# Two transformer blocks on one core: when the scatter of an expert's output runs among the next experts' matmuls

## The chip, the cores and the metric

The kernel runs on one core of one Trainium2 chip. Its time is that of one execution on the device, in microseconds. Three executions were timed; the trace is of the one that took longest.

## What is computed

Two blocks in a row work on 256 tokens of width 1024, all in float32. The first has two mixers and a mixture of 16 experts, the second attention and two dense feed-forward parts. Only the experts matter here:

```python
for e in range(N_EXPERTS):                  # 16
    a = jax.nn.silu(t @ w_gate[e]) * (t @ w_up[e])
    y = y + combine[:, e:e + 1] * (a @ w_down[e]).astype(f32)
```

`t` is 256 × 1024, `w_gate[e]` and `w_up[e]` are 1024 × 512, `w_down[e]` is 512 × 1024. Each token is routed to 2 of the 16 experts; `combine` is zero for the others.

## The kernel before

**Precision.** A float32 product is made of products of parts. Each weight is split into `w_hi` (rounded, by ScalarE, `split_hi`) and `w_lo` (the rest, by VectorE, `split_lo`); activations are split in the same way.

**Units.** Weights arrive in units of 128 × 2048 values (1 MB) in one order: per expert two for the gate, two for up, and two for down, which stand one expert later. `w_raw` has 6 buffers, `w_hi` and `w_lo` have 3 each (`SPLIT`). So ScalarE can split a unit only when TensorE has used the unit three before it (`unit_used`). TensorE then waits for `lo_ready`.

**Few tokens.** Where every expert has at most 64 tokens the kernel takes the branch `few_experts`, and it does so here. Per expert 64 columns of tokens are gathered, and their high and low parts stand side by side, so that a unit (`unit_few`) is eight matmuls of 128 × 128 by 512: four with `w_hi` (line 1922) and four with `w_lo` (line 1923).

**One pass of the loop on TensorE**, for expert `e`, in order:

1. four units, gate, gate, up, up (called here the first to the fourth unit);
2. the fold of the gate rows (line 1948), which turns them and adds their two parts;
3. the first half of the down product of expert `e-1`, one unit;
4. the fold of the up rows;
5. the transposes that make `pickT` and the weights of `e` (lines 1940 and 1942), and a gather (line 1934) for later experts;
6. the second half of the down product of `e-1`, one unit, which waits until VectorE has read the first half from the same PSUM bank (`y_half_lo`);
7. another gather, and then the scatter of `e-1`.

The scatter (`scatter`, line 1968) multiplies the output rows of an expert, `y_hi` and `y_lo`, by `pickT` and adds them to the tokens' sums in four PSUM banks. It is two halves of four matmuls by 512 columns. Each half waits for `y_half_lo` of its half.

**The other engines.** ScalarE and VectorE have written-out orders of their own, `few_experts` too. On ScalarE, behind the second down unit of `e-1`: `y_hi` of its second half (line 726), the split of the next expert's third unit (line 505), `aT_hi` (line 715), the copy of the gathered rows (line 692). The next pass's first unit waits for that copy (`gath_set`). On VectorE `y_lo` (line 1311) stands between two splits (line 898). `y_hi` and `y_lo` have one buffer for each half: the scatter of `e-1` must be over before the first down unit of `e`, whose end lets ScalarE write them again.

Of the kernel before, what the change touches and what calls it, by code (L numbers as in the profile page):

```python
# [32 lines left out]
N_EXP = GROUPS * PER_GROUP  # L33
# [78 lines left out]
def two_blocks_kernel(nc, a, out):  # L112
# [7 lines left out]
    with ExitStack() as ctx:  # L120
# [76 lines left out]
        def pair_rows(e):  # L197

            buf = h_hi if (e // 2) % 2 == 0 else h_lo
            return buf[:, :, :].rearrange("p k (e m) -> p k e m", e=2)[:, :, e % 2, :]  # L200
# [10 lines left out]
        def u_in(e, j):  # L211
            return U_MOE + j if e == 0 else U_MOE + 4 + STEP * (e - 1) + j
# [1419 lines left out]
        def _(pe):  # L1632
# [284 lines left out]
            def unit_few(u, bank, rows, k0, first, last):  # L1917

                pe.wait_ge(lo_ready, u + 1)
                for k in range(4):  # L1920
                    wc = slice(k * 512, k * 512 + 512)
                    pe.matmul(ps[:, bank, :], rows[:, k0 + k, :], w_hi[:, u % SPLIT, wc], start=first and k == 0, stop=False)  # L1922
                    ins = pe.matmul(ps[:, bank, :], rows[:, k0 + k, :], w_lo[:, u % SPLIT, wc], start=False, stop=last and k == 3)  # L1923
                ins.then_inc(unit_used, 1)

            def gather(n):

                pair = pick[:, :, 2 * (n // 4):2 * (n // 4) + 2, 0:SLOTS]
                for k in range(2):
                    o = ps[:, chunk_bank(n), 256 * k:256 * k + 256].rearrange("p (e l s) -> p l e s", e=2, l=2)  # L1930
                    c = slice((2 * (n % 4) + k) * P, (2 * (n % 4) + k + 1) * P)
                    for part, h2 in enumerate((h2_hi, h2_lo)):
                        for tt in range(TT):
                            ins = pe.matmul(o[:, part], h2[:, tt, c], pair[:, tt], start=(tt == 0), stop=(tt == 1))
                ins.then_inc(gathered, 1)

            def transpose_pick(e):

                for tt in range(TT):
                    pe.transpose(ps[:, B_GATE, tt * P:(tt + 1) * P], pick_f[:, tt, e, :], ident)  # L1940
                for tt in range(TT):
                    ins = pe.matmul(ps[:, B_GATE, S:S + 1], pick_f[:, tt, e, :], comb[:, tt, e:e + 1], start=(tt == 0), stop=(tt == 1))
                ins.then_inc(pick_T, 1)

            def fold_rows(rows, c0):

                for f in range(4):
                    ins = pe.matmul(ps[:, B_T, c0 + SLOTS * f:c0 + SLOTS * (f + 1)], rows[:, f * P:(f + 1) * P], fold, start=True, stop=True)  # L1948
                ins.then_inc(aT_done, 1)

            def down_few(e, half):

                if half:
                    pe.wait_ge(y_half_lo, 2 * e + 1)
                else:
                    pe.wait_ge(aT_lo_r, 2 * (e + 1))
                    if e:
                        pe.wait_ge(y_half_lo, 2 * e)
                unit_few(u_down(e, half), B_Y, aT_hi[:, :, 0:P], 0, True, True)

            def scatter(e, half):

                pe.wait_ge(y_half_lo, 2 * e + (half + 1))
                pe.wait_ge(pickT_set, e + 1)
                for tt in range(TT):
                    o = ps[:, 4 + 2 * half + tt, :]
                    for n, y in enumerate((y_hi, y_lo)):
                        ins = pe.matmul(o, pickT[:, e, tt * P:(tt + 1) * P], y[:, 512 * half:512 * half + 512],  # L1968
                                        start=(e == 0 and n == 0), stop=(e == N_EXP - 1 and n == 1), skip_group_check=True)
                ins.then_inc(y_used, 1)  # L1970

            def few_experts():

                pe.wait_ge(h2_lo_set, 2)
                pe.wait_ge(fold_set, 1)
                pe.wait_ge(pick_ready, 1)
                for n in range(4):
                    gather(n)
                for e in range(N_EXP):
                    rows = pair_rows(e)  # L1980
                    if e == 0:
                        pe.wait_ge(gath_set, 2)
                    else:
                        pe.wait_ge(gath_set, 4 + 2 * min(e, N_EXP - 2))
                        pe.wait_ge(pickT_set, e)
                        pe.wait_ge(slot_w_set, e)
                    unit_few(u_in(e, 0), B_GATE, rows, 0, True, False)
                    if e == 0:
                        pe.wait_ge(gath_set, 4)
                    unit_few(u_in(e, 1), B_GATE, rows, 4, False, True)  # L1990
                    unit_few(u_in(e, 2), B_UP, rows, 0, True, False)
                    unit_few(u_in(e, 3), B_UP, rows, 4, False, True)
                    if e:
                        pe.wait_ge(a_done, e)
                    pe.wait_ge(gate_kept, e + 1)
                    fold_rows(gate_rows, 0)
                    if e:
                        down_few(e - 1, 0)
                    pe.wait_ge(up_kept, e + 1)
                    fold_rows(up_rows, 4 * SLOTS)  # L2000
                    if e == 0:
                        pe.wait_ge(pick_ready, 2)
                    transpose_pick(e)
                    if e < N_EXP - 2:
                        gather(4 + 2 * e)
                    if e:
                        down_few(e - 1, 1)
                    if e < N_EXP - 2:
                        pe.wait_ge(pickT_set, e + 1)
                        pe.wait_ge(slot_w_set, e + 1)  # L2010
                        gather(5 + 2 * e)
                    if e:
                        scatter(e - 1, 0)
                        scatter(e - 1, 1)
                down_few(N_EXP - 1, 0)
                down_few(N_EXP - 1, 1)
                scatter(N_EXP - 1, 0)
                scatter(N_EXP - 1, 1)
# [5 lines left out]
            with pe.If(is_few > 0):  # L2024
                few_experts()
# [326 lines left out]
```

## Time and profile before

| | us |
|---|---|
| three timed runs | 1186.71, 1187.0, 1191.82 |
| their median | 1187.0 |
| the profiled execution, one of the three | 1191.82 |
| its span in the profile | 1189.8 |
| TensorE busy | 1082.2 (91%) |
| VectorE busy | 733.6 (62%) |
| ScalarE busy | 616.8 (52%) |
| mean granted TensorE clock, share of full | 0.945 |

The span is the time from the first to the last instruction that the profiler recorded. Times in the trace count from its start. The stage of the experts lies from about 280 to 604 us. TensorE's busy time counts each matmul from its start to its modelled end, and matmuls overlap: one of 512 columns is shown with 0.39 us, while the next starts 0.23 us after it. So distances from start to start say more than busy time. In the timeline PE is a matmul, PEld the load of its stationary operand, and the bracket gives how long the engine was idle before it and what ended that.

### The profile page before, as it was taken

The numbers are of one execution on the slowest core, as the hardware profiler recorded it, in microseconds if no ns is written. First come the engines' busy times: TensorE is split into PE (matmuls) and PEld (weight loads), VectorE is DVE, ScalarE is ACT, GpSimd is POOL, SyncE is SP. The second block draws the span as 40 slices with busy tenths as digits, with TensorE's granted clock in tenths as the row PEclk, the third lists the DMA queues.
The fourth block names the chain that finished last, engine by engine and source line by source line (L and its number), as shares of the span: only waits on it lengthen the run. The fifth ranks groups of instructions, "written<-read, shape, count | busy, mean of one in ns | idle before, by whom it ended". The sixth has DMA issues, their size and how long they took to land.

```text
span 1189.8 us, 14176 instructions
## 1 busy us (share of the span) xinstructions
PE 1082.2 (91%) x5471; PEld 897.4 (75%) x5471; DVE 733.6 (62%) x821; ACT 616.8 (52%) x721; POOL 56.4 (5%) x47
## 2 busy tenths in 40 slices
PE   5999999887999999999869999987999799999997
PEld 4788888676777777777657888876878677788886
DVE  5434685557678787878764655554556645555654
ACT  5466533345777877777644334333554425344331
POOL 0000561020000000000000000000000000000000
PEclk8999998887999999999889999997998969999999
DMA  7843442343789898989848556552520015555520
GB/s 265 300 142 110 138 142 89 123 149 111 277 319 325 313 336 306 340 306 341 303 152 302 191 181 201 187 177 71 175 73 2 1 36 172 182 178 192 193 72 36
DMA packets 116993, 223.34 MB, mean 188 GB/s; under 512 B 6402, under 2 KB 12681, under 8 KB 116938
## 3 DMA queue, kind: packets, MB, share of 16 engines
q1 hardware_dynamic: 112846, 216.77, 53.0%
q10 hardware_dynamic: 3708, 4.57, 1.1%
q0 software_dynamic: 384, 1.24, 0.3%
q8 instruction: 38, 0.62, 0.2%
q14 instruction: 17, 0.14, 0.0%
HBM read 221.49 MB, written 1.07 MB: 187 GB/s over the span
## 4 chain that ended last, share of the span: by engine, by line
PE 75%; DVE 13%; ACT 7%; issue 3%; ACTq 1%; DMA 0%; DVEq 0%
PE ps L1650 17%; PE ps L1651 16%; PE ps L1652 16%; DVE w_lo L898 7%; PE ps L1922 5%; ACT w_hi L505 4%; PE ps L1923 4%; PE ps L1948 2%; PE ps L2155 2%; PE ps L1968 2%; PE ps L1792 1%; DVE y_lo L1311 1%; ACT y_hi L726 1%; PE ps L2118 1%; DVE h_lo L925 1%
## 5 line engine op out<-in xcount | busy, mean ns | idle before, releaser
L898 DVE TENSOR_TENSOR w_lo<-w_raw,w_hi 128x2048 fp32r<-128x2048 f32 x204 | 465.3, 2290 | 170.6 <-ACT w_hi L505 169.4
L505 ACT ACTIVATE w_hi<-w_raw 128x2048 fp32r<-128x2048 f32 x204 | 388.1, 1913 | 257.1 <-PE ps L1652 208.4
L1650 PE MATMUL ps<-w_hi,h_hi 128*128 128x512 f32 (+1 forms) x704 | 276.0, 392 | 13.4 <-DVE h_lo L925 7.7
L1651 PE MATMUL ps<-w_lo,h_hi 128*128 128x512 f32 (+1 forms) x704 | 271.3, 385 | 0.0
L1652 PE MATMUL ps<-w_hi,h_lo 128*128 128x512 f32 (+1 forms) x704 | 271.2, 385 | 0.0
L1650 PEld LDWEIGHTS ps<-w_hi,h_hi 128*128 128x128 f32 x704 | 135.3, 192 | 41.6 <-DVE h_lo L925 8.6
L1652 PEld LDWEIGHTS ps<-w_hi,h_lo 128*128 128x128 f32 x704 | 134.8, 191 | 26.5
L1651 PEld LDWEIGHTS ps<-w_lo,h_hi 128*128 128x128 f32 x704 | 135.1, 192 | 24.5
L1650 PE MATMUL ps<-w_hi,aT_hi 128*128 128x512 f32 x192 | 77.3, 403 | 7.7 <-DVE aT_lo L1223 6.0
L1651 PE MATMUL ps<-w_lo,aT_hi 128*128 128x512 f32 x192 | 76.7, 400 | 0.0
L1652 PE MATMUL ps<-w_hi,aT_lo 128*128 128x512 f32 x192 | 76.6, 399 | 0.0
L1922 PE MATMUL ps<-w_hi,aT_hi 128*128 128x512 f32 x128 | 54.5, 426 | 9.6 <-DVE y_lo L1311 8.3
L1922 PE MATMUL ps<-w_hi,h_hi 128*128 128x512 f32 x128 | 53.7, 419 | 6.6 <-DVE w_lo L898 5.9
L1922 PE MATMUL ps<-w_hi,h_lo 128*128 128x512 f32 x128 | 51.8, 405 | 5.8 <-DVE w_lo L898 5.8
L1923 PE MATMUL ps<-w_lo,h_hi 128*128 128x512 f32 x128 | 51.9, 405 | 0.0
L1923 PE MATMUL ps<-w_lo,aT_hi 128*128 128x512 f32 x128 | 51.8, 405 | 0.0
L1923 PE MATMUL ps<-w_lo,h_lo 128*128 128x512 f32 x128 | 50.1, 392 | 0.0
L1650 PEld LDWEIGHTS ps<-w_hi,aT_hi 128*128 128x128 f32 x192 | 37.4, 195 | 16.1 <-issue 8.2
L1311 DVE SCALAR_TENSOR_TENSOR y_lo<-ps,scalars,y_hi 128x512 fp32r<-128x512 f32 x32 | 23.9, 748 | 38.9 <-ACT y_hi L726 38.8
L861 ACT ACTIVATE arena<-arena,scalars 128x128 f32<-128x128 f32 (+1 forms) x64 | 26.1, 409 | 40.1 <-DVE scalars L1536 39.8
L1232 DVE SCALAR_TENSOR_TENSOR x_res<-ps,scalars,x_res 128x512 f32<-128x512 f32 x48 | 33.7, 745 | 19.8 <-PE ps L1652 19.8
L1652 PEld LDWEIGHTS ps<-w_hi,aT_lo 128*128 128x128 f32 x192 | 37.2, 194 | 8.0
(315 smaller groups left out, 1380.7 us busy)
## 6 DMA issues: line engine op xcount, KB each, us to landing
w_raw<-in_ffn_w_in SPq DMA_DIRECT2D x44, 1024.0 KB, 5.1
w_raw<-in_w_exp_gate SPq DMA_DIRECT2D x32, 1024.0 KB, 5.3
w_raw<-in_w_exp_up SPq DMA_DIRECT2D x32, 1024.0 KB, 6.4
w_raw<-in_w_exp_down SPq DMA_DIRECT2D x32, 1024.0 KB, 7.1
w_raw<-in_w_in SPq DMA_DIRECT2D x22, 1024.0 KB, 6.7
w_raw<-in_ffn_w_out SPq DMA_DIRECT2D x22, 1024.0 KB, 5.0
w_raw<-in_w_mix_in SPq DMA_DIRECT2D x8, 1024.0 KB, 5.2
w_raw<-in_w_out SPq DMA_DIRECT2D x4, 1024.0 KB, 5.0
```

The lines of the kernel that those rows point to most:

```text
L505: act.activation(w_hi[:, u % SPLIT, :], w_raw[:, u % RAW, :], ACT.Copy).then_inc(hi_ready, 1)
L861: i = act.activation(w[:, cs], w[:, cs], ACT.Exp, scale=-1.0, bias=negm[:, k:k + 1], accum_out=sums[:, k:k + 1])
L898: dve.tensor_tensor(w_lo[:, u % SPLIT, :], w_raw[:, u % RAW, :], w_hi[:, u % SPLIT, :], ALU.subtract).then_inc(lo_ready, 1)
L1232: dve.scalar_tensor_tensor(out=x[:, tt, cs], in0=ps[:, 4 + 2 * half + tt, :], scalar=coef[:, tt:tt + 1], in1=x[:, tt, cs], op0=ALU.mult, o ...
L1311: dve.scalar_tensor_tensor(out=y_lo[:, cs], in0=ps[:, B_Y, :], scalar=slot_w[:, e:e + 1], in1=y_hi[:, cs], op0=ALU.mult, op1=ALU.subtract) ...
L1650: pe.matmul(out, hi, w_h, start=first, stop=False)
L1651: pe.matmul(out, hi, w_l, start=False, stop=False)
L1652: return pe.matmul(out, lo, w_h, start=False, stop=last)
L1922: pe.matmul(ps[:, bank, :], rows[:, k0 + k, :], w_hi[:, u % SPLIT, wc], start=first and k == 0, stop=False)
L1923: ins = pe.matmul(ps[:, bank, :], rows[:, k0 + k, :], w_lo[:, u % SPLIT, wc], start=False, stop=last and k == 3)
L1948: ins = pe.matmul(ps[:, B_T, c0 + SLOTS * f:c0 + SLOTS * (f + 1)], rows[:, f * P:(f + 1) * P], fold, start=True, stop=True)
L1968: ins = pe.matmul(o, pickT[:, e, tt * P:(tt + 1) * P], y[:, 512 * half:512 * half + 512], start=(e == 0 and n == 0), stop=(e == N_EXP - 1 ...
```

## The change

The scatter of an expert is issued in another place on TensorE. Before, the pass of expert `e` ended with the scatter of `e-1`. Now the pass of `e`, from expert 2 on, has the scatter of `e-2` between its third and fourth unit. The last two scatters stand where they were. Nothing else is changed: the other engines' orders are the same.

```diff
@@ -1989,6 +1989,9 @@
                         pe.wait_ge(gath_set, 4)
                     unit_few(u_in(e, 1), B_GATE, rows, 4, False, True)
                     unit_few(u_in(e, 2), B_UP, rows, 0, True, False)
+                    if e >= 2:
+                        scatter(e - 2, 0)
+                        scatter(e - 2, 1)
                     unit_few(u_in(e, 3), B_UP, rows, 4, False, True)
                     if e:
                         pe.wait_ge(a_done, e)
@@ -2009,9 +2012,8 @@
                         pe.wait_ge(pickT_set, e + 1)
                         pe.wait_ge(slot_w_set, e + 1)
                         gather(5 + 2 * e)
-                    if e:
-                        scatter(e - 1, 0)
-                        scatter(e - 1, 1)
+                scatter(N_EXP - 2, 0)
+                scatter(N_EXP - 2, 1)
                 down_few(N_EXP - 1, 0)
                 down_few(N_EXP - 1, 1)
                 scatter(N_EXP - 1, 0)
```

The first place is TensorE at the end of expert 1's pass. The gather reads `pick`, the scatter reads `y_hi`, `y_lo` and `pickT`, and `w_hi`, `w_lo` with `h_lo` is the first unit of expert 2 (its token columns lie in `h_lo`). Before:

```order
L1934 MATMUL ps<-pick,h_hi 128x2x64 x2
L1934 MATMUL ps<-pick,h_lo 128x2x64 x2
L1968 MATMUL ps<-y_hi,pickT 128x512 [waits pickT_set,y_half_lo]
L1968 MATMUL ps<-y_lo,pickT 128x512
L1968 MATMUL ps<-y_hi,pickT 128x512
L1968 MATMUL ps<-y_lo,pickT 128x512
L1968 MATMUL ps<-y_hi,pickT 128x512 [waits pickT_set,y_half_lo]
L1968 MATMUL ps<-y_lo,pickT 128x512
L1968 MATMUL ps<-y_hi,pickT 128x512
L1968 MATMUL ps<-y_lo,pickT 128x512
L1922 MATMUL ps<-w_hi,h_lo 128x512 [waits slot_w_set,lo_ready,pickT_set,gath_set]
L1923 MATMUL ps<-w_lo,h_lo 128x512
```

After:

```order
L1934 MATMUL ps<-pick,h_hi 128x2x64 x2
L1934 MATMUL ps<-pick,h_lo 128x2x64 x2
L1922 MATMUL ps<-w_hi,h_lo 128x512 [waits slot_w_set,lo_ready,pickT_set,gath_set]
L1923 MATMUL ps<-w_lo,h_lo 128x512
L1922 MATMUL ps<-w_hi,h_lo 128x512
```

The eight matmuls of the scatter are gone from here, and the first unit follows the gather.

The second place is TensorE in expert 2's pass, where its third unit ends and its fourth begins. Before:

```order
L1922 MATMUL ps<-w_hi,h_lo 128x512
L1923 MATMUL ps<-w_lo,h_lo 128x512
L1922 MATMUL ps<-w_hi,h_lo 128x512 [waits lo_ready]
L1923 MATMUL ps<-w_lo,h_lo 128x512
L1922 MATMUL ps<-w_hi,h_lo 128x512
```

After, from the end of the third unit:

```order
L1922 MATMUL ps<-w_hi,h_lo 128x512
L1923 MATMUL ps<-w_lo,h_lo 128x512
L1968 MATMUL ps<-y_hi,pickT 128x512 [waits pickT_set,y_half_lo]
L1968 MATMUL ps<-y_lo,pickT 128x512
L1968 MATMUL ps<-y_hi,pickT 128x512
L1968 MATMUL ps<-y_lo,pickT 128x512
L1968 MATMUL ps<-y_hi,pickT 128x512 [waits pickT_set,y_half_lo]
L1968 MATMUL ps<-y_lo,pickT 128x512
L1968 MATMUL ps<-y_hi,pickT 128x512
L1968 MATMUL ps<-y_lo,pickT 128x512
L1922 MATMUL ps<-w_hi,h_lo 128x512 [waits lo_ready]
L1923 MATMUL ps<-w_lo,h_lo 128x512
```

The scatter of expert 0 now stands ahead of the fourth unit. It carries its two waits along.

## Rows read from the trace of the kernel before

**Rows 1.** The page, parts 1 and 4: busy share, and the chain by engine

```profile
PE 1082.2 (91%) x5471; PEld 897.4 (75%) x5471; DVE 733.6 (62%) x821; ACT 616.8 (52%) x721; POOL 56.4 (5%) x47
...
PE 75%; DVE 13%; ACT 7%; issue 3%; ACTq 1%; DMA 0%; DVEq 0%
```

**Rows 2.** Waits, 320 to 600 us: total, times, longest

```profile
ACT w_hi L505 <- PE ps L1923: 31.2, 14, 2.3
PEld ps L1922 <- DVE w_lo L898: 16.6, 15, 1.2
...
PEld ps L1968 <- DVE y_lo L1311: 11.5, 14, 0.9
```

**Rows 3.** Timeline, expert 8, first to fourth unit: start, us, engine, operation, idle

```profile
436.25 0.50 PE L1922 MATMUL ps<-w_hi,h_hi 128*128 128x512 f32 x1
...
438.46 1.92 ACT L505 ACTIVATE w_hi<-w_raw 128x2048 fp32r<-128x2048 f32 x1 [2.26 <-PE ps L1923]
...
440.01 0.39 PE L1922 MATMUL ps<-w_hi,h_hi 128*128 128x512 f32 x1
...
440.41 6.78 DVE L898 TENSOR_TENSOR w_lo<-w_raw,w_hi 128x2048 fp32r<-128x2048 f32 x3 [0.63 <-ACT w_hi L505]
...
441.60 0.39 PE L1923 MATMUL ps<-w_lo,h_hi 128*128 128x512 f32 x1
...
442.75 0.50 PE L1922 MATMUL ps<-w_hi,h_hi 128*128 128x512 f32 x1 [0.77 <-DVE w_lo L898]
...
443.09 0.40 PE L1923 MATMUL ps<-w_lo,h_hi 128*128 128x512 f32 x1
```

**Rows 4.** Timeline, expert 8, behind the fourth unit

```profile
448.49 0.38 ACT L708 ACTIVATE arena<-ps 128x256 f32<-128x256 f32 x1 [1.18 <-PE ps L1948]
...
449.49 0.75 DVE L1311 SCALAR_TENSOR_TENSOR y_lo<-ps,scalars,y_hi 128x512 fp32r<-128x512 f32 x1 [2.31 <-ACT y_hi L726]
...
450.29 0.50 PE L1922 MATMUL ps<-w_hi,aT_hi 128*128 128x512 f32 x1 [0.32 <-DVE y_lo L1311]
...
452.44 0.69 ACT L726 ACTIVATE y_hi<-ps,scalars 128x512 fp32r<-128x512 f32 x1 [0.43 <-PE ps L1923]
```

**Rows 5.** Timeline, end of expert 8's pass and start of expert 9's

```profile
453.03 1.91 ACT L505 ACTIVATE w_hi<-w_raw 128x2048 fp32r<-128x2048 f32 x1
453.08 0.44 PE L1968 MATMUL ps<-y_hi,pickT 128*128 128x512 f32 x1
...
455.14 0.59 ACT L692 ACTIVATE h_lo<-ps 128x512 fp32r<-128x512 f32 x1
...
455.44 0.40 PE L1968 MATMUL ps<-y_lo,pickT 128*128 128x512 f32 x1
455.78 0.19 PEld L1922 LDWEIGHTS ps<-w_hi,h_hi 128*128 128x128 f32 x1 [0.38 <-ACT h_lo L692]
...
457.03 2.28 DVE L898 TENSOR_TENSOR w_lo<-w_raw,w_hi 128x2048 fp32r<-128x2048 f32 x1
```

**Rows 6.** Chain of work, 450 to 460 us: start, us, what

```profile
454.63 1.20 PE ps L1968 x4
```

**Rows 7.** Timeline, expert 15: `w_lo` of the third unit, load of the fourth

```profile
574.85 2.29 DVE L898 TENSOR_TENSOR w_lo<-w_raw,w_hi 128x2048 fp32r<-128x2048 f32 x1
...
579.89 0.19 PEld L1922 LDWEIGHTS ps<-w_hi,h_lo 128*128 128x128 f32 x1 [1.00 <-DVE w_lo L898]
```

**Rows 8.** Stretches: length, then busy us by engine, granted clock (PEclk), DMA, GB/s

```profile
core 0: us, PE busy (x) PEld busy (x) DVE busy (x) ACT busy (x) POOL busy (x), PEclk, DMA share, GB/s
320.00:560.00 240.00, 221.40 (x1150) 178.15 (x1149) 192.29 (x137) 186.90 (x184) 0.00 (x0) 1.00 0.90 324
564.40:567.80 3.40, 2.13 (x18) 1.96 (x17) 1.08 (x2) 2.24 (x4) 0.00 (x0) 1.00 1.02 345
567.90:571.20 3.30, 3.30 (x10) 2.52 (x9) 2.36 (x2) 1.05 (x3) 0.00 (x0) 0.50 0.79 304
```

**Rows 9.** Timeline, TensorE, expert 14: second down unit into the scatter

```profile
567.45 0.50 PE L1922 MATMUL ps<-w_hi,aT_hi 128*128 128x512 f32 x1 [1.27 <-DVE y_lo L1311]
...
571.43 0.40 PE L1968 MATMUL ps<-y_hi,pickT 128*128 128x512 f32 x1
```

## The prediction, made before the result was known

> **What bounds the kernel now.** I read the page first: TensorE is busy 91% of the span and carries 75% of the chain that ended last, so a change of its order can matter at all [rows 1]. Busy matmuls overlap here, so I read steps from start to start and not busy time. The change touches only the stage of the 16 experts, so next I read the waits of its even part, 320 to 600 us. Everything there waits in small amounts for everything else: ScalarE 31.2 us in 14 pieces for TensorE before a weight split, TensorE's weight loads 16.6 us in 15 pieces for VectorE's `w_lo`, and 11.5 us in 14 pieces at the scatter for `y_lo` [rows 2]. That is a loop through three engines, and its period is 19.53 us: expert 8's first unit starts at 436.25 us and expert 9's at 455.78 us [rows 3, 5]. So I walked one lap of it in the timeline.
>
> First quarter [rows 3]. A matmul follows the one before by 0.227 us (third unit: first at 440.01, eighth at 441.60). TensorE could go on at 441.83, but the fourth unit starts at 442.75: its weights come from ScalarE's split (start 438.46, 1.92 us), which had waited 2.26 us for the first unit to free one of three buffers, and VectorE's (start 440.41, three in 6.78 us, so the first ends near 442.7). There is a hole of 0.92 us on TensorE. This is where the scatter is put.
>
> Middle [rows 4]. The fourth unit is followed by the fold of the gate rows, a down unit and the fold of the up rows, one behind the other. ScalarE waits 1.18 us for this last one (448.49), then VectorE's `y_lo` (449.49) releases the second down unit at 450.29, and ScalarE waits 0.43 us for that one before `y_hi` at 452.44. So from the fourth unit on, each link waits for the one before: TensorE, ScalarE, VectorE, TensorE, ScalarE. What delays the fourth unit delays all.
>
> End [rows 5]. Behind `y_hi` ScalarE has no idle time: a weight split at 453.03, `aT_hi`, the copy of gathered rows at 455.14 for 0.59 us, so until 455.73. The first unit starts at 455.78, and its weight load, idle for 0.38 us, is put down to this copy. In the same time TensorE does the scatter, 453.08 to 455.44 by starts, free at 455.67. The scatter and ScalarE's three instructions lie beside each other, and ScalarE's ends last, by 0.06 us. The chain of work instead names four scatter matmuls, 1.20 us from 454.63, ahead of the first unit [rows 6]: it is a near tie, and the chain takes the other arm.
>
> **The change part by part.** *Removed behind the gathers, 14 times:* eight matmuls and, before the fifth, a wait for `y_lo` (11.5 us over 14 passes, 0.8 us each [rows 2]). What then sets the first unit? The copy at 455.73, whose inputs (the gather, done before the scatter, and `aT_hi`) don't depend on the scatter. Gain 0; at most 0.05 us a pass, if the load of weights hides better. VectorE is a second wall there: the third unit's `w_lo` starts at 457.03 and takes 2.28 us [rows 5], to 459.31, and the third unit would start at 455.78 + 2 × 1.82 + 0.11 = 459.5. No large gain lies behind the copy.
>
> *Added ahead of the fourth unit, 14 times:* its waits (`y_lo`, `pickT` of two experts back) are long fulfilled, so no wait is added. Eight matmuls at 0.227 are 1.82 us. The hole covers 0.92, so the fourth unit starts 0.90 us later. Against that the first matmul after a stall holds the second back to 0.34 us (442.75 to 443.09) where 0.23 is usual [rows 3]; without a stall 0.11 comes back. 0.79 us a pass. Bounds: 0 (if later links had slack) and 1.82 (no cover). Behind the fourth unit are queued both folds, both down units and both gathers, all of which wait in turn by [rows 4]: I find no slack, and take 0.79.
>
> *The last of the 14* (expert 14 to 15) has no gathers, so no copy holds the first unit, which can come up to 2 us earlier. But the third unit's `w_lo` still starts at 574.85 and takes 2.29 us, to 577.14; with the third unit and the scatter (2 × 1.82) the fourth starts at 580.8 where it started at 579.89 [rows 7]. 0.9 us later there too, 0.8 after the stall's 0.11. Sum of the order alone: 14 × 0.79 = 11.1 us.
>
> *The clock.* The removal leaves TensorE from about 453.1 to 455.78 without work, 2.7 us, behind eight small gather matmuls. No even pass has such a stretch now, and the granted clock is 1.00 from 320 to 560 us. What a thin stretch does can be seen in passes 14 and 15: from 564.4 to 567.8 TensorE had 18 matmuls, 2.13 us busy, most of them small; then the clock fell to 0.50, the lower of its two levels, 1.2 of 2.4 GHz, for 567.9 to 571.2 [rows 8]. Pass 15 shows the same again. The new stretch is thinner than those (the fold and the transposes there, eight gathers here). A fall costs: from 567.45 to 571.43 ten steps took 3.98 us, and at 0.227 plus the 0.11 they take 2.4, so 1.6 us [rows 9]. It would hit the first, second and third unit; now that TensorE and not `w_lo` sets the fourth, all of it counts. How often is not in this trace: 0 to 14. Both thin stretches named brought a fall, but the nearest thing to them in the even passes (fold, transposes and gathers, up to the second down unit at 450.29 [rows 4]) brought none, so a thin stretch alone doesn't settle it. I take 6, under half: 6 × 1.6 = 9.6 us. The bounds are 0 and 22.
>
> Beside this row stands a rule of the Trainium skill, "TensorE: Matmul & The Clock Gate", section "A second HAM failure mode: psum-queue depth-cycling": short idles between groups of matmuls let the clock swing between its levels, and the re-warming costs throughput. It speaks against this change, and the trace agrees with it at 567.9 us. Held to strictly, it gives a fall in every pass and 1187 + 11 + 22 = 1220 us; without it the sum is 1198.
>
> *Nothing else moves.* VectorE, ScalarE and the DMA queue keep their order. Loads get 0.8 us more time a pass.
>
> **Sum.** 11.1 + 9.6 = 20.7 us. The profiled execution took 1191.8 us (span 1189.8) and would take 1212.5. It is the highest of three runs; the median, 1187.0, is 4.8 lower, so 1207.7, say 1207.5.
>
> **The rivals.**
> 1. *No further clock falls*: 1187.0 + 11.1 = 1198. For it: the granted clock is 1.00 in all even passes. Against: no even pass has such an empty stretch. Chance 0.27.
> 2. *A fall nearly each pass*, or falls that last twice as long: 12 or more falls, 1187.0 + 11.1 + 19 = 1217 and up. Chance 0.08.
> 3. *No change*, the delay is swallowed: ScalarE waits 2.26 + 1.18 + 0.43 = 3.9 us a pass [rows 3, 4], which looks like slack. But all of it is ScalarE waiting for TensorE, not the reverse. It would give 1187. Chance 0.04.
> 4. *Faster, by the chain of work*: the scatter is what held the first unit, which starts earlier once that is gone. The place is the end of the lap, the price is what VectorE's wall leaves: the third unit no earlier than 459.31, and the fourth unit's `w_lo` 2.2 us behind it, at 461.6 where it comes 442.75 + 19.53 = 462.3. 0.7 us a pass, 14 × 0.7 = 10 us, 1177. It decides only if the scatter takes under 0.92 us in its new place, and it takes 1.82; and if the copy at 455.73 isn't the releaser. Chance 0.03.
>
> **How the numbers follow.** The forecast (order plus some falls, 1202 to 1216) has 0.58, rivals 0.27, 0.08, 0.04 and 0.03. The range runs from just below rival 1 to the forecast's upper end, 1197 to 1216.5: it leaves out rivals 2 to 4 and some of the edges. About 0.5% (6 us) is what a measurement of this kernel tells from no change. Slower by more has 0.58 + 0.27 + 0.08 = 0.93, within 0.5% 0.04, faster 0.03.
>
> **What the changed profile would show.** Scatter rows right behind the third unit without a wait, fourth unit 0.9 us later after the first than now (7.4 for 6.5 us), without idle time in front of it; a hole of 2.6 us before each first unit, put down to ScalarE's copy; a period of 20.3 us in passes without a fall; and slices at 320 to 600 us with granted clock below 1.00 and passes of 21.5 to 22 us. I am wrong on the order if the period stays at 19.5, and on the clock if it stays 1.00. A first unit that starts well before the copy's end would mean that I misread the tie.

## The result, and the profile after

| | before | changed |
|---|---|---|
| runs beside each other, us | 1186.71, 1187.0, 1191.82, 1199.11 | 1210.27, 1212.5, 1212.8, 1214.58 |
| median | 1189.41 | 1212.65 |
| profiled execution | 1191.82 | 1210.27 |
| span in the profile | 1189.8 | 1208.3 |

The change makes the kernel slower: the ratio is 1.0154, 95% interval 1.0115 to 1.0192. The forecast was 1207.5 us, in a range of 1197 to 1216.5.

The page of the changed kernel, parts 1 and 4, to compare with [rows 1]:

```profile
PE 1077.9 (89%) x5471; PEld 903.4 (75%) x5471; DVE 734.8 (61%) x821; ACT 617.8 (51%) x721; POOL 55.8 (5%) x47
...
PE 81%; DVE 8%; ACT 6%; issue 3%; ACTq 1%; DMA 0%; DVEq 0%
```

The same work, 18.5 us more of span. In the chain VectorE fell from 13% to 8% and TensorE rose from 75% to 81%: where the fourth unit had waited for VectorE's `w_lo`, the chain now runs through TensorE's matmuls.

The timeline of one pass, from expert 6's first unit to expert 7's. It answers to [rows 3] and [rows 5]:

```profile
398.98 0.50 PE L1922 MATMUL ps<-w_hi,h_lo 128*128 128x512 f32 x1 [2.53 <-ACT h_lo L692]
...
404.36 0.40 PE L1923 MATMUL ps<-w_lo,h_lo 128*128 128x512 f32 x1
404.59 0.39 PE L1968 MATMUL ps<-y_hi,pickT 128*128 128x512 f32 x1
...
406.41 0.39 PE L1922 MATMUL ps<-w_hi,h_lo 128*128 128x512 f32 x1
...
416.41 0.38 PE L1934 MATMUL ps<-pick,h_lo 128*128 128x128 f32 x2
419.31 0.50 PE L1922 MATMUL ps<-w_hi,h_lo 128*128 128x512 f32 x1 [2.52 <-ACT h_hi L692]
```

The scatter follows the third unit at the usual step. The fourth unit comes at 406.41, 7.43 us behind the first, where it was 442.75 - 436.25 = 6.50 us [rows 3]. The next first unit comes at 419.31, so the pass takes 20.33 us for 19.53. In front of both first units stands a hole of 2.5 us, put down to ScalarE's copy. The last gather matmuls start at 416.41, and TensorE then has nothing until ScalarE has done its split (416.57), `aT_hi` and the copy (418.68).

The chain of work of the changed kernel, 410 to 425 us, to compare with [rows 6]:

```profile
416.57 1.90 ACT w_hi L505
418.47 0.30 ACT aT_hi L715
418.77 0.50 ACT h_hi L692
...
419.31 0.50 PE ps L1922
```

The arm that the chain named before, four scatter matmuls behind VectorE's `y_lo`, is gone, and its place has ScalarE's split, `aT_hi` and copy. They end as late as ever: from `y_hi` to the first unit it is 419.31 - 415.98 = 3.33 us, and before 455.78 - 452.44 = 3.34 us [rows 4, 5]. The scatter's removal gained nothing.

Now the clock. The timeline of ScalarE in the changed kernel, the last copy of gathered rows of four passes in a row, shows their lengths. The view below it has stretches with their granted clock (PEclk, third number from the end):

```profile
418.68 0.59 ACT L692 ACTIVATE h_hi<-ps 128x512 fp32r<-128x512 f32 x1
...
439.01 0.59 ACT L692 ACTIVATE h_hi<-ps 128x512 fp32r<-128x512 f32 x1
...
462.13 0.59 ACT L692 ACTIVATE h_lo<-ps 128x512 fp32r<-128x512 f32 x1
...
484.01 0.59 ACT L692 ACTIVATE h_lo<-ps 128x512 fp32r<-128x512 f32 x1
```

```profile
320.00:435.00 115.00, 100.42 (x543) 85.43 (x543) 85.91 (x60) 86.97 (x84) 0.00 (x0) 1.00 0.88 314
438.90:445.50 6.60, 5.85 (x14) 4.60 (x15) 4.31 (x4) 2.61 (x3) 0.00 (x0) 0.50 0.92 328
...
462.80:466.00 3.20, 3.20 (x8) 2.52 (x9) 3.20 (x3) 0.00 (x0) 0.00 (x0) 0.50 0.96 340
316.00:319.20 3.20, 3.01 (x7) 2.43 (x8) 3.20 (x3) 0.14 (x1) 0.00 (x0) 0.50 0.99 326
565.20:571.80 6.60, 5.82 (x14) 4.56 (x15) 4.31 (x3) 2.64 (x3) 0.00 (x0) 0.50 1.00 326
```

From last copy to last copy (418.68, 439.01, 462.13, 484.01) the passes are 20.33, 23.12 and 21.88 us. In the two long ones TensorE ran at 0.50, the lower level, from 438.9 to 445.5 and from 462.8 to 466.0, right behind the hole. From 320 to 435 us, with the same hole in each pass, the clock stayed at 1.00. So a fall costs 1.55 us, or 2.79 where it lasts 6.6 us. The stage has two more, one at 316 us and a long one at 565.2; before had two single ones in it, at 567.9 and 588.4 us.

The timeline of TensorE at the first of these, to compare with [rows 9]:

```profile
436.74 0.38 PE L1934 MATMUL ps<-pick,h_lo 128*128 128x128 f32 x2
439.65 0.80 PE L1922 MATMUL ps<-w_hi,h_hi 128*128 128x512 f32 x1 [2.52 <-ACT h_hi L692]
440.24 0.63 PE L1923 MATMUL ps<-w_lo,h_hi 128*128 128x512 f32 x1
...
445.36 0.52 PE L1923 MATMUL ps<-w_lo,h_hi 128*128 128x512 f32 x1
445.72 0.40 PE L1922 MATMUL ps<-w_hi,h_hi 128*128 128x512 f32 x1
```

One matmul of 512 columns every 0.43 us instead of 0.23, from 440.24 to 445.36.

The sum over the stage, from the last copy of expert 1's pass to VectorE's first addition of the expert sums. Before:

```profile
318.37 0.59 ACT L692 ACTIVATE h_lo<-ps 128x512 fp32r<-128x512 f32 x1
...
601.83 1.22 DVE L1339 TENSOR_TENSOR x_res<-ps,x_res 128x1024 f32<-128x1024 f32 x1
```

After:

```profile
315.55 0.59 ACT L692 ACTIVATE h_lo<-ps 128x512 fp32r<-128x512 f32 x1
...
618.03 1.22 DVE L1339 TENSOR_TENSOR x_res<-ps,x_res 128x1024 f32<-128x1024 f32 x1
```

283.5 us before and 302.5 us after, 19.0 more. The rest of the span took 0.5 less: 2.8 less ahead of this stretch and 2.3 more behind it, where nothing was changed. Fourteen insertions at 0.80 are 11.2, so 7.8 us are left for the clock: four falls, two of them long, in place of two.

By the passes the four cost 8.6: the pass at 316 us took 21.79 us, 1.46 over 20.33, and from expert 14's first unit to its fourth it took 10.19 us, 2.76 over 7.43; with 2.79 and 1.55 that is 8.56. So the two falls of before cost only about 0.8 together. One of them can be read in the fourth units of experts 14 and 15. Before:

```profile
559.91 0.50 PE L1922 MATMUL ps<-w_hi,h_lo 128*128 128x512 f32 x1 [0.77 <-DVE w_lo L898]
```

After, with expert 15's first unit between them:

```profile
576.17 0.39 PE L1922 MATMUL ps<-w_hi,h_lo 128*128 128x512 f32 x1
...
587.36 0.47 PE L1922 MATMUL ps<-w_hi,h_lo 128*128 128x512 f32 x1 [1.66 <-DVE w_lo L898]
...
596.44 0.39 PE L1922 MATMUL ps<-w_hi,h_lo 128*128 128x512 f32 x1
```

Before, it was 19.98 us with a fall, to 579.89 [rows 7]; after, 20.27 without one, of which 0.80 are the insertion's. By this the fall cost 0.5 us there, and the fourth unit behind it still waited 0.56 us for `w_lo`. In the changed kernel no such wait is left, and a single fall costs all of its 1.5.

These are two executions. The medians lie 23.2 us apart, and the one profiled is the fastest of the changed kernel's four. The other three have a lower mean granted clock, 0.936 to 0.939 for 0.943; where their falls lie no trace shows.

### The profile page after: what moved, and what is told of

Read it like the earlier page. It is cut to its first block, busy times and chain, and to the rows that moved or that the text cites. A ratio compares the mean times of both kernels' runs of the same rounds, so it can differ in the third digit from the quotient of the medians.

```text
span 1208.3 us, 14176 instructions
## 1 busy us (share of the span) xinstructions
PE 1077.9 (89%) x5471; PEld 903.4 (75%) x5471; DVE 734.8 (61%) x821; ACT 617.8 (51%) x721; POOL 55.8 (5%) x47
## 4 chain that ended last, share of the span: by engine, by line
PE 81%; DVE 8%; ACT 6%; issue 3%; ACTq 1%; DMA 0%; DVEq 0%
PE ps L1650 17%; PE ps L1651 16%; PE ps L1652 16%; PE ps L1922 8%; PE ps L1923 7%; ACT w_hi L505 4%; PE ps L1968 2%; PE ps L1948 2%; DVE w_lo L898 2%; PE ps L2157 2%; PE ps L1792 1%; DVE y_lo L1311 1%; ACT y_hi L726 1%; PE ps L2120 1%; DVE h_lo L925 1%
## 5 line engine op out<-in xcount | busy, mean ns | idle before, releaser
L1652 PEld LDWEIGHTS ps<-w_hi,h_lo 128*128 128x128 f32 x704 | 135.2, 192 | 26.7
L1650 PE MATMUL ps<-w_hi,aT_hi 128*128 128x512 f32 x192 | 75.8, 395 | 7.7 <-DVE aT_lo L1223 6.0
L1651 PE MATMUL ps<-w_lo,aT_hi 128*128 128x512 f32 x192 | 75.2, 392 | 0.0
L1922 PE MATMUL ps<-w_hi,aT_hi 128*128 128x512 f32 x128 | 53.4, 417 | 9.7 <-DVE y_lo L1311 8.3
L1923 PE MATMUL ps<-w_lo,aT_hi 128*128 128x512 f32 x128 | 50.4, 394 | 0.0
L1922 PEld LDWEIGHTS ps<-w_hi,h_lo 128*128 128x128 f32 x128 | 25.6, 200 | 28.4 <-ACT h_lo L692 10.7
```

The lines of the kernel that those rows point to most:

```text
L1650: pe.matmul(out, hi, w_h, start=first, stop=False)
L1651: pe.matmul(out, hi, w_l, start=False, stop=False)
L1652: return pe.matmul(out, lo, w_h, start=False, stop=last)
```

## Experiments

All times are medians; each ratio is that of runs of the experiment to runs of the kernel before on the same chip, with its 95% interval. A pass is the distance between last copies, and 12 of them lie between experts 1 and 13. Where an experiment adds a line above a place, that place has a higher line number.

### 1. Is the scatter free in its old place? Most of it left out there

```diff
--- kernel before
                     for n, y in enumerate((y_hi, y_lo)):
+                        if 0 < e < N_EXP - 1 and (tt, n) != (1, 1):
+                            continue
                         ins = pe.matmul(o, ...
```

> The kernel before, with the scatter in its old place but only one matmul in four of it for experts 1 to 14: 84 matmuls of 0.227 us, 19.1 us of TensorE work, are left out (their part of the sum is missing). Theory (the scatter's old place was free, ScalarE's copy of gathered rows sets the first unit): the passes between the copies keep 19.5 us where the clock is 1.00, nothing is gained by the order, and since the hole before the first unit grows to about 2 us some clock falls come, so the time is 1187 to 1205. Rival (the chain of work: the scatter sets the first unit): passes of 18.6 to 19.1 us, 1175 to 1182.

Measured: 1207.05 us against 1193.7, ratio 1.0124 (1.0088 to 1.016). The range was made for a kernel before of 1187 us, and there the ratio is 1201.7. Nineteen microseconds of matmuls are gone, and the kernel is slower. Timeline of ScalarE's last copies in this run, and its stretch of 320 to 560 us:

```profile
355.09 0.58 ACT L692 ACTIVATE h_hi<-ps 128x512 fp32r<-128x512 f32 x1
...
374.60 0.58 ACT L692 ACTIVATE h_lo<-ps 128x512 fp32r<-128x512 f32 x1
...
395.65 0.58 ACT L692 ACTIVATE h_lo<-ps 128x512 fp32r<-128x512 f32 x1
```

```profile
320.00:560.00 240.00, 206.56 (x1044) 166.94 (x1042) 184.10 (x131) 181.53 (x180) 0.00 (x0) 0.96 0.89 311
```

A pass without a fall is 19.51 us (355.09 to 374.60) as before, with 1.4 us less of TensorE work in it; six of the twelve are like that (19.51 to 19.56). The next has a fall and takes 21.05, and so do the other five, with 20.95 to 21.08. So the scatter held nothing up in its old place: the chain's arm through it was one of two equal ones. And its matmuls kept the clock up: without them it is 0.96 on the mean of the stretch, where it was 1.00 [rows 8]. Nothing of the changed kernel's order is in this run, only a hole, in two pieces of 1.1 and 0.6 us, the second put down to ScalarE's copy. The rival (1175 to 1182 us) is out.

### 2. The clock's part: the hole filled with matmuls of no use

```diff
--- changed kernel
+            def filler(e):
+                pe.wait_ge(gath_set, 5 + 2 * e)
+                for n in range(8):
+                    pe.matmul(ps[:, B_UP, :], pickT[:, e, 0:P],
+                              h_hi[:, 0:2, :].rearrange("p k m -> p (k m)"), start=True, stop=True)
...
                         gather(5 + 2 * e)
+                        if e:
+                            filler(e)
```

> The changed kernel, with eight matmuls of 512 columns without use issued behind the second gather, in the hole of 2.6 us that the scatter left (experts 1 to 13). Theory (order costs 0.8 us a pass, the hole brings clock falls on top): passes stay at 20.3 us although TensorE has 1.8 us more work each, no fall between 320 and 560 us, and the time is that of before plus 10 to 12 us, 1198 to 1202. Rival (the falls have another cause, or cost nothing): as the changed kernel, 1210 to 1214; or 1225 and more if the eight matmuls lie on the path.

Measured: 1205.8 us, ratio 1.0108 (1.0079 to 1.0137), which on 1187 us is 1199.8, inside what was expected. The changed kernel's ratio of 1.0154 was taken beside other runs of the kernel before (median 1189.41, here 1193.7), and the two intervals overlap, so times alone don't part them. The passes and the clock do:

```profile
355.12 0.59 ACT L692 ACTIVATE h_hi<-ps 128x512 fp32r<-128x512 f32 x1
...
375.48 0.58 ACT L692 ACTIVATE h_lo<-ps 128x512 fp32r<-128x512 f32 x1
```

```profile
320.00:560.00 240.00, 228.78 (x1207) 191.21 (x1206) 183.81 (x130) 179.86 (x178) 0.00 (x0) 1.00 0.87 309
```

20.36 us a pass, clock 1.00 over the whole stretch, and no pass there longer than 20.42 us. TensorE does 23.6 us (13 × 8 × 0.227) of work for nothing, and the falls of the stretch are gone. What is left, 0.8 us a pass, is the order alone.

### 3. Only as much as the hole before the fourth unit holds

```diff
--- kernel before
                     unit_few(u_in(e, 2), B_UP, rows, 0, True, False)
+                    if e >= 2:
+                        scatter(e - 2, 1)
                     unit_few(u_in(e, 3), B_UP, rows, 4, False, True)
...
-                    if e:
+                    if 1 <= e < N_EXP - 1:
                         scatter(e - 1, 0)
-                        scatter(e - 1, 1)
+                scatter(N_EXP - 2, 0)
+                scatter(N_EXP - 2, 1)
```

> The scatter is split: its first half stays behind the gathers, its second half (0.91 us) goes between the third and fourth unit of the next pass, whose hole is 0.92 us. Theory (what exceeds the hole costs): the fourth unit is not delayed, passes of 19.5 us, no gain; with a hole of 1.8 us before the first unit a few clock falls may come, so 1186 to 1196. Rival (any scatter there delays the splits or the folds): passes of 20 us and more, 1195 to 1200. Rival (waiting for the second half of y_lo at the end of a pass was the cost): passes under 19.2 us, 1180 or less.

Measured: 1198.88 us, ratio 1.0041 (1.0018 to 1.0064), on 1187 us 1191.9.

```profile
376.62 0.59 ACT L692 ACTIVATE h_lo<-ps 128x512 fp32r<-128x512 f32 x1
...
396.20 0.59 ACT L692 ACTIVATE h_lo<-ps 128x512 fp32r<-128x512 f32 x1
```

376.62 to 396.20 is 19.58 us, and the ten passes without a fall take 19.53 to 19.58, for 19.53 before: four matmuls fit into 0.92 us and cost at most 0.05. The other four, at the end of a pass, gained nothing by standing alone, although the wait for the second half of `y_lo` was gone: the first unit waits 1.56 us for ScalarE's copy. Two passes of 21.0 and 21.1 us have the clock's fall, 3.0 us together, of the 5.2 by which the medians differ. So the hole holds four matmuls for next to nothing, and eight cost the difference.

### 4. ScalarE's copy earlier, scatter in its old place

```diff
--- kernel before, ScalarE
                     if e:
                         y_out(e - 1, 1)
-                        split_hi(s + 8)
                     a_few(e)
                     if e < N_EXP - 2:
                         gather_out(5 + 2 * e)
+                    if e:
+                        split_hi(s + 8)
```

> The kernel before, with one change on ScalarE: the copy of the gathered rows (and aT_hi) stands ahead of the split of the next third unit, so it ends about 1.8 us earlier. Theory (copy and scatter end within 0.06 us of each other, so now the scatter alone sets the first unit): the first unit gains at most 0.1 to 0.2 us, passes of 19.35 to 19.5 us, 1184 to 1188; the first unit's wait is no longer put down to the copy. Rival (something else on ScalarE or VectorE sets the pass): 1187 or, if the later split holds the third unit, 1190 and more.

Measured: 1191.45 us, ratio 0.9983 (0.9965 to 1.0), on 1187 us 1185.0. The passes are 19.29 to 19.35 us, at or just under the forecast:

```profile
371.60 0.59 ACT L692 ACTIVATE h_lo<-ps 128x512 fp32r<-128x512 f32 x1
...
390.93 0.59 ACT L692 ACTIVATE h_lo<-ps 128x512 fp32r<-128x512 f32 x1
```

TensorE, the second half of the scatter in the same pass:

```profile
392.22 0.50 PE L1969 MATMUL ps<-y_hi,pickT 128*128 128x512 f32 x1 [0.41 <-DVE y_lo L1312]
```

With the copy out of the way by 1.8 us, the first unit gains 0.2: it starts at 393.25, the usual step behind the scatter's last matmul (393.02), so the scatter was right behind. The two arms were a tie, as read. And what holds the scatter is VectorE: its second half waits 0.41 us for `y_lo`.

### 5. The same on the changed kernel

> The changed kernel with ScalarE's copy ahead of the split of the next third unit, as in the third-from-last edit on the kernel before. Theory (VectorE's w_lo of the third unit is the second wall): the first unit starts some 1.8 us earlier and the hole in front of it shrinks below 1 us, so no clock falls between 320 and 560 us; but the third unit can't start earlier and the scatter is still between it and the fourth, so the passes stay between 20.3 and 20.5 us: before plus 11 to 14 us, a ratio of 1.009 to 1.012. Rival (the copy was all that held the changed order back): passes of 19.3 us or less, the time of before or better.

Measured: 1205.75 us, ratio 1.0104 (1.0072 to 1.0136). The edit is that of experiment 4, made to the changed kernel (the expectation's "third-from-last edit" is that one). Timeline of TensorE, the first matmuls of the first, second and third unit with the wait ahead of each:

```profile
377.66 0.47 PE L1923 MATMUL ps<-w_hi,h_hi 128*128 128x512 f32 x1 [0.81 <-ACT h_lo L692]
...
380.43 0.50 PE L1923 MATMUL ps<-w_hi,h_hi 128*128 128x512 f32 x1 [0.69 <-DVE w_lo L899]
...
382.96 0.50 PE L1923 MATMUL ps<-w_hi,h_hi 128*128 128x512 f32 x1 [0.43 <-DVE w_lo L899]
```

20.26 to 20.34 us a pass, and no fall from 320 to 560 us. The hole in front of the first unit is now 0.81 us, but the second unit waits 0.69 us and the third 0.43 us for `w_lo`. VectorE's splits are the second wall, where they were put. What the scatter gave up in front of the first unit can't be collected even with the copy moved, and between the third and fourth unit it still costs.

### 6. Both walls moved, scatter in its old place

```diff
--- experiment 4, VectorE
                     split_lo(s + 5)
+                    split_lo(s + 6)
                     if e:
                         y_out_lo(e - 1, 0)
                     gated_few(e)
                     slot_w_out(e)
-                    split_lo(s + 6)
```

> The kernel before, scatter in its old place, with two changes of order off TensorE: ScalarE's copy of gathered rows first (as in the run with that change alone), and on VectorE the split of the next first unit ahead of y_lo, in the 2.3 us that VectorE waits for y_hi. Theory (ScalarE's copy and VectorE's splits are the walls behind the down units): both recede, passes of 18.5 to 18.7 us, before minus 9 to 14 us, ratio 0.988 to 0.992. Rival (the hole before the fourth unit sets the pass whatever stands behind it): 19.3 us as with the copy alone. Rival (the loads, at 0.9 of the DMA engines' time, become the bound): passes of 19 us with waits for w_raw.

Measured: 1185.08 us against 1193.93, ratio 0.993 (0.9906 to 0.9954), just short of the forecast, as are the passes of 18.69 to 18.74 us:

```profile
372.75 0.59 ACT L692 ACTIVATE h_lo<-ps 128x512 fp32r<-128x512 f32 x1
...
391.44 0.59 ACT L692 ACTIVATE h_lo<-ps 128x512 fp32r<-128x512 f32 x1
```

```profile
320.00:560.00 240.00, 226.38 (x1192) 185.34 (x1191) 200.60 (x140) 194.14 (x190) 0.00 (x0) 0.99 0.94 337
```

The split of the next first unit fills the time in which VectorE waited for `y_hi` [rows 4]. The chain of work of the kernel before shows where it had stood: ahead of `y_lo`, for which the scatter's second half waits (454.63 in [rows 6]):

```profile
451.72 2.20 DVE w_lo L898
453.91 0.67 DVE y_lo L1311
```

Now the eight matmuls of the scatter run through without that wait, from 391.19 to 392.88 by starts. Of the 0.8 us a pass that this kernel gains, 0.2 came with experiment 4's edit and 0.6 with this one. It is faster than both kernels. The loads moved 337 GB/s, and no engine waited for `w_raw` between 320 and 560 us.

### 7. The same with half of the scatter in the hole

> As the run with both changes of order off TensorE, and the scatter's second half between the third and fourth unit of the next pass. Theory (the hole before the fourth unit is still about 0.65 us and takes most of it; the end of the pass gets shorter by the other half): passes of 18.7 to 18.9 us, no better than with both changes and the old place. Rival (with the walls gone, moving part of the scatter into the hole pays): passes of 18.2 us or less.

The edits are those of experiments 3 and 6. Measured: 1180.88 us, ratio 0.9904 (0.987 to 0.9938). It is the fastest median here. By the passes it is not better than experiment 6, as expected:

```profile
370.87 0.59 ACT L692 ACTIVATE h_lo<-ps 128x512 fp32r<-128x512 f32 x1
...
389.63 0.59 ACT L692 ACTIVATE h_lo<-ps 128x512 fp32r<-128x512 f32 x1
```

370.87 to 389.63 is 18.76 us, for 18.69 to 18.74. The times of both overlap by their intervals, and my forecast "no better" fails by the medians. Passes don't explain the 4 us. Half of it lies ahead of them in the profiles: the copy that ends the same pass stands at 370.87 us here and at 372.75 in experiment 6, while nothing ahead of the stage differs between the two kernels. In the ten profiles of this document the stage's first copy stands at 272.9 to 274.1 us in six and at 276.0 to 276.5 in four, the kernel before among these, and all ten are the same up to there, so it is the execution's. At least that half isn't the edit's; the rest is open.

### 8. Another place among the four units

```diff
--- changed kernel
                     unit_few(u_in(e, 0), B_GATE, rows, 0, True, False)
+                    if e >= 2:
+                        scatter(e - 2, 0)
+                        scatter(e - 2, 1)
...
                     unit_few(u_in(e, 2), B_UP, rows, 0, True, False)
-                    if e >= 2:
-                        scatter(e - 2, 0)
-                        scatter(e - 2, 1)
```

> The changed kernel with the scatter of two experts back between the first and second unit instead of the third and fourth. Theory one (only the hole before the fourth unit counts, wherever in the four units the scatter stands): passes of 20.3 us, as in the changed kernel. Theory two (the second unit's end frees the buffer for the split of the first down unit, which VectorE then delivers late, so a scatter ahead of the second unit costs more): passes of 20.8 to 21.1 us, before plus 20 us and more.

Measured: 1237.11 us, ratio 1.0387 (1.0349 to 1.0424). Theory two holds:

```profile
521.65 0.58 ACT L692 ACTIVATE h_hi<-ps 128x512 fp32r<-128x512 f32 x1
...
542.58 0.59 ACT L692 ACTIVATE h_hi<-ps 128x512 fp32r<-128x512 f32 x1
```

521.65 to 542.58, a pass without a fall, is 20.93 us. In front of the second unit the scatter also delays the second unit's end, and with it the splits of the down units. TensorE, the first matmul of the first down unit:

```profile
532.96 0.47 PE L1922 MATMUL ps<-w_hi,aT_hi 128*128 128x512 f32 x1 [0.44 <-DVE w_lo L898]
```

From the first unit to the fold of the gate rows it is 9.2 us as in the changed kernel (522.29 to 531.52, there 398.98 to 408.24). The down unit comes 1.44 us behind that, for 0.81 there: this wait is the 0.6 us a pass in which the two differ. Most other passes in this run have a fall and take 22.3 to 23.7 us.

## Why the prediction was right

**The tie at the end of a pass** was read rightly. I took the copy's end at 455.73 over the scatter's at 455.67 against what the chain of work named. Experiment 1 shows it: without most of the scatter the pass stays at 19.5 us. Experiment 4 shows the other side, 0.2 us with the copy gone.

**The hole before the fourth unit** was read rightly, 0.92 us. For what exceeds it the forecast was 0.79 us a pass, and it is 0.80 (20.33 for 19.53). Half a scatter fits, experiment 3.

**No slack behind the fourth unit**: also right, the delay came through to the next first unit whole. The wait at the scatter's fifth matmul, put at 0.8 us, is that of its weight load; the matmul itself stands idle for 0.40. No term of the sum hangs on it.

**VectorE as the second wall** was argued and is shown by experiment 5. In the changed kernel the copy binds first, except in expert 15's pass, which has no copy: there the first three units wait for `w_lo` (1.66, 0.69 and 0.43 us), the wall that the prediction named for that pass.

**The clock** was right in kind. The term was 9.6 us (six falls at 1.6 beyond those of before), and 7.8 is what the stage leaves over the order. That these two lie near each other is partly luck. There were two falls more than before and not six. But two of the four came twice as long, at 2.8 us, which I had as part of rival 2, and the two of before had cost 0.8 together, so that more was added than their number says. That all of a fall would count, now that `w_lo` no longer sets the fourth unit, was right: 1.55 us for a single one. Experiment 2 takes them away and leaves the passes at 20.36 us, and experiment 1 brings them to the kernel before. How many come in a run was an assumption and stays one: in the changed kernel some equal passes have one and others don't, in one and the same execution. The rule of the Trainium skill that I set beside it ("TensorE: Matmul & The Clock Gate", "A second HAM failure mode: psum-queue depth-cycling") is borne out in kind by experiments 1 and 2. Held to strictly, a fall in every pass, it is not: 320 to 435 us has none.

**The total**: 1207.5 forecast, 1212.65 measured, inside the range, and 20.7 us more forecast for 23.2 by the medians, 18.5 by the profiled spans. Of the 5 us between them, 2.4 lie in the kernel before, whose median is 1189.4 here and not 1187.0; against that median the forecast would be 1209.9.

**Rival 1** (no falls, 1198) is out by the profile. **Rival 3** is out, ScalarE's waits were no slack for TensorE. **Rival 4** (faster) fails twice, by the copy and by the eight matmuls that take 1.82 us in a hole of 0.92.

## What to carry to other kernels

Before you move work out of the way of something, look for the second engine that ends beside it. The chain of work shows one arm of a tie; take the end of each engine's last instruction before the wait, and what is left when the first arm is gone. A hole takes as much as it is long, and the rest is paid in every pass of a loop that has no slack behind it. And work that costs nothing may keep TensorE's clock up: what is left where it stood belongs in the sum.

## What the runs showed that I had not expected

Leaving out 19 us of matmuls made the kernel 1.2% slower (experiment 1), and adding 23.6 us of useless ones took away all falls between 320 and 560 us (experiment 2). A fall may last 6.6 us and then costs 2.8. And a scatter ahead of the second unit costs 1.4 us a pass, against 0.8 ahead of the fourth.
